# Forgetting attention in a Macaron layer: weight splits moved to the long tiles, a key split in two, and one row of the last stage reordered

## The chip, the cores and the metric

The kernel runs on one core of a Trainium2 chip. The metric is the device time of one execution in microseconds. The program has five engines with a queue of instructions each: PE (TensorE, matmul), DVE (VectorE), ACT (ScalarE), POOL (GpSimd) and SP (SyncE, which here only issues DMAs). Every order below is written out by hand, and the engines meet at semaphores.

## The reference

One layer on 1024 tokens of width 1024, all in float32: a feed-forward block (SwiGLU, inner width 2816), a mixer, a cross attention to 256 memory rows, and a second feed-forward block, each between two RMS norms and with a residual, then a last RMS norm. Half of the mixer is the forgetting attention (8 heads of 64):

```python
def forgetting_attention(q, k, v, log_f):
    qf = (q.astype(F32) * (dh ** -0.5)).transpose(0, 2, 1, 3)
    c = jnp.cumsum(log_f, axis=1).transpose(0, 2, 1)
    for i in range(S // Q_BLOCK):
        s = jnp.einsum('bhqd,bhkd->bhqk', qf[:, :, q0:L], kf[:, :, :L])
        s = s + c[:, :, q0:L, None] - c[:, :, None, :L]
        p = jax.nn.softmax(jnp.where(mask, s, -jnp.inf), axis=-1)
        outs.append(jnp.einsum('bhqk,bhkd->bhqd', p, vf[:, :, :L]))
```

The last block ends with `x = x + 0.5 * rms_norm(y, g_ff2_post)` and `return rms_norm(x, g_final)`.

## The kernel before

Products in float32 are made of three products of rounded parts: a tensor is split into a high part (ACT copies it into the rounded type) and a low part (DVE subtracts the high part from the source). `high_s(n)` (line 952; its copy is line 993) and `low_s(n)` (line 2004; line 2013) do this for the n-th piece of the weights, and `low_s` frees the raw tile that SP then reloads (`load_s`, line 512).

**Attention.** The 8 heads are done in four pairs (`attend_fox(p)`, p = 0 to 3, one function for each engine). A pair has 16 tiles, one for each head of the pair and block of 128 queries, in the order of `FOX_ORDER` (line 36). A tile of block b has (b + 1) x 128 keys, so tiles 0 to 5 are short (128 to 512 keys), 6 to 10 are mixed (640, 384, 768, 512, 896), and 11 to 15 have 640 to 1024. Tile a goes through the engines so: PE makes the scores (lines 1462 to 1465), DVE takes their maximum (line 2058), ACT the exponential with its sum (line 1066), PE transposes the probabilities (line 1476), DVE copies the first four transposed blocks out (line 2072) and ACT the others (line 1073), PE multiplies with the values (line 1487), and DVE scales the result (reciprocal line 2062, product line 2077). In PE's step a stand, in this order, the scores of tile a, the transposes of a - 1, and the values of a - 2; the scores of tile a wait for the exponential of a - 2, because two pairs of PSUM banks are used in turn. In DVE's step a stand the maximum of a, the reciprocal for a - 3, then the copy of a - 1 and the scaling of a - 3.

Into this are woven, for each pair: the second half (keys 512 to 1023) of the pair's keys, whose low parts DVE makes in `keep_q` in step 4 (lines 2029 and 2030, one for each head) and signals on `proj_dve`, for which PE's scores of tile 6 wait (line 1449); the copy of one of these parts, `keep_k1`, in step 7 (line 2037), needed from tile 11 on; and the split of two weight pieces for the next pair, ACT's in steps 4 and 6 and DVE's in steps 6 and 8. PE needs these weights for the projections of the next pair, after its scores of tile 15.

**The last stage.** `ff_2(1)` adds the last products of the second feed-forward block tile by tile (eight tiles of 128 tokens). For tile s of step s, DVE adds the product (`add_y`, line 1934), ACT sums the squares (line 810), POOL makes the root (`root1`, lines 649 and 651), DVE scales by it and adds the old row (`scale_y`, lines 1826 and 1830), ACT sums squares again (line 821), POOL makes the second root (`root2`, lines 656 and 658), and DVE makes the output row (`make_row`, line 1841), which SP sends (line 630). The rows stand in two buffers in turn. `make_row(4, i)` waits for the output of tile i - 2 to have landed (line 1838). DVE's queue in step s is `add_y(s)`, `scale_y(s - 1)`, `make_row(s - 2)`.

Of the kernel before, what the change touches and what calls it, by code (L numbers as in the profile page):

```python
# [7 lines left out]
ALU = mybir.AluOpType  # L8
# [8 lines left out]
NT = T // P  # L17
# [49 lines left out]
S_FV, S_SMALL, S_Q, S_GQ, S_GV, S_GR, S_OUT = 0, 4, 5, 13, 17, 21, 25  # L67
# [41 lines left out]
def build_layer(nc, x, mem, g_ff1_pre, w_ff1_gate, w_ff1_up, w_ff1_down, g_ff1_post,  # L109
# [4 lines left out]
    with ctx:  # L114
# [27 lines left out]
        ps = ctx.enter_context(nc.psum_tensor("ps", [P, 8, HT], F32))  # L142
# [82 lines left out]
        def f32(ap):  # L225
            return ap.bitcast(F32)
# [80 lines left out]
        ka = [at_kb(f"ka{i}", (172, 168)[i], [P, T], F32R) for i in range(2)]  # L307
# [70 lines left out]
        proj_done, proj_dve, proj_act = sem("proj_done"), sem("proj_dve"), sem("proj_act")  # L378
# [417 lines left out]
        def _(act):  # L796
# [248 lines left out]
            def attend_fox(p):  # L1045
                splits = {4: S_Q + 2 + 2 * p, 6: S_Q + 3 + 2 * p}
                for a in range(17):
# [4 lines left out]
                    if a < 16:  # L1052
# [12 lines left out]
                        bank = 2 * (a % 2)  # L1065
# [750 lines left out]
        def _(dve):  # L1816
            ve = nc.vector
# [155 lines left out]
            def ff_2(f):  # L1973
                bd = 1 + 3 * f
# [19 lines left out]
                for s in range(NT + 3):  # L1994
                    if s < NT:
                        add_y(f, NG[f] - 1, s)
                    if 1 <= s <= NT:
                        scale_y(bd, s - 1)
                    if 2 <= s <= NT + 1:
                        make_row(bd, s - 2)  # L2000
                    if f == 0 and s >= 3:
                        low_h(bd, s - 3)
# [12 lines left out]

            def keep_q(n, t, bank):
                dve.wait_ge(proj_done, event(n, t))
# [10 lines left out]
                else:  # L2028
                    ve.tensor_tensor(ka[0][upper, c], ps[lower, bank + t, :], f32(ka[0][lower, c]), ALU.subtract)
                    op = ve.tensor_tensor(ka[1][lower, c], ps[upper, bank + t, :], f32(ka[1][upper, c]), ALU.subtract)  # L2030
                op.then_inc(proj_dve, 1)

# [17 lines left out]
            def attend_fox(p):  # L2050
                splits = {6: S_Q + 2 + 2 * p, 8: S_Q + 3 + 2 * p}
                for a in range(19):
# [7 lines left out]
                    if a >= 3:  # L2060
                        h3, b3 = FOX_ORDER[a - 3]
                        ve.reciprocal(row_inv[:, b3, h3:h3 + 1], row_sum[:, b3, h3:h3 + 1])
                    if a == 4:
                        keep_q(S_Q + 2 * p + 1, 1, 2 if p else 0)
                    if a == 7:
                        keep_k1(p, 1)
# [322 lines left out]
```

## Time and profile before

| | |
|---|---|
| runs | 2337.10, 2337.19, 2345.70 us; median 2337.19 |
| profiled execution | 2339.64 us, of which its span (first to last instruction) 2337.9 us |
| PE busy | 2246.3 us, 96% |
| DVE, ACT, POOL busy | 1117.1 us (48%), 791.0 us (34%), 468.4 us (20%) |
| mean granted clock of PE | 0.979 of 2.4 GHz |
| attention, four pairs | 813.74 to 1074.90 us |
| last stage, tail after the last matmul | 2323.5 to 2337.9 us |

Times in the rows are microseconds from the first instruction of the profiled execution. A row of the timeline gives the start, the duration, engine, line, operation and tiles, and in brackets how long the engine had been idle before it and what ended that. A duration can overlap that of the next row, since the engines are pipelined. A row of a table by stretches gives the stretch, its length, the busy time (and instructions) of PE, of PE's weight loads, of DVE, ACT and POOL, the granted clock of PE (1.00 is 2.4 GHz, 0.50 is 1.2 GHz), the share of the DMA engines and GB/s.

### The profile page before, as it was taken

To read this page: it belongs to the slowest core of one execution; us is meant where nothing else is said; L and a number is where in the kernel's file an instruction comes from. 1 tells how busy PE (TensorE), PEld (TensorE's weight loads), DVE (VectorE), ACT (ScalarE), POOL (GpSimd) and SP (SyncE) were. 2 spreads that over 40 slices of the span, in tenths; PEclk is the share of its full clock that TensorE was granted. 3 is DMA by queue.
4 is the path that set the end of the run, shared out by engine and by line. 5 is a ranking of instruction groups with operands and counts; after the bars stand their busy time and mean duration, and the time that the engine had idled before them with its cause. 6 is when DMAs were issued, how large, how long until landed. Compare 5 with 4: busy or idle time off the path is not lost. (4 is left out here: it accounts for less than half of the span.)

```text
span 2337.9 us, 27140 instructions
## 1 busy us (share of the span) xinstructions
PE 2246.3 (96%) x10640; PEld 1849.0 (79%) x10640; DVE 1117.1 (48%) x1389; ACT 791.0 (34%) x1242; POOL 468.4 (20%) x447
## 2 busy tenths in 40 slices
PE   5999999999999999999999999999699999999997
PEld 4788888888887788888777787778588888888886
DVE  7544444464456354552245543144744444454446
ACT  6433333331124533441222343244533333332113
POOL 2343434300012000000131100001343444410003
PEclk8999999999999996999999999999899999999998
DMA  3222222253333000001131161032122222243323
GB/s 117 91 90 72 90 72 90 73 182 98 117 89 113 19 19 19 20 19 54 55 108 55 58 208 53 16 126 81 45 91 72 90 72 90 79 144 120 117 81 126
DMA packets 105856, 195.01 MB, mean 83 GB/s; under 512 B 8129, under 2 KB 73682, under 8 KB 102914
## 3 DMA queue, kind: packets, MB, share of 16 engines
q1 hardware_dynamic: 105730, 193.27, 25.8%
q8 instruction: 86, 1.41, 0.2%
q14 instruction: 40, 0.33, 0.0%
HBM read 153.34 MB, written 39.91 MB: 83 GB/s over the span
## 5 line engine op out<-in xcount | busy, mean ns | idle before, releaser
L1357 PE MATMUL ps<-xc,wg 128*128 128x512 f32 x1232 | 484.6, 393 | 28.3 <-DVE xc L1892 24.4
L1359 PE MATMUL ps<-xc,wg 128*128 128x512 f32 x1232 | 483.4, 392 | 0.0
L1358 PE MATMUL ps<-xc,wg 128*128 128x512 f32 x1232 | 483.3, 392 | 0.0
L1357 PEld LDWEIGHTS ps<-xc,wg 128*128 128x128 f32 x1232 | 233.9, 190 | 80.4 <-issue 21.9
L1375 PE MATMUL ps<-d_w,d_hid 128*128 128x512 f32 x704 | 274.5, 390 | 2.9 <-DVE d_w L1924 2.8
L1377 PE MATMUL ps<-d_w,d_hid 128*128 128x512 f32 x704 | 273.9, 389 | 0.0
L1376 PE MATMUL ps<-d_w,d_hid 128*128 128x512 f32 x704 | 273.9, 389 | 0.0
L1359 PEld LDWEIGHTS ps<-xc,wg 128*128 128x128 f32 x1232 | 233.5, 189 | 49.1
L1358 PEld LDWEIGHTS ps<-xc,wg 128*128 128x128 f32 x1232 | 233.9, 190 | 48.5
L1898 DVE TENSOR_TENSOR wg<-w_sums,wg 128x1024 fp32r<-128x1024 f32 x88 | 124.1, 1410 | 189.3 <-ACT wg L857 189.3
L1934 DVE TENSOR_TENSOR y<-y,ps 128x1024 f32<-128x1024 f32 x88 | 107.4, 1220 | 215.1 <-PE ps L1377 215.1
L1375 PEld LDWEIGHTS ps<-d_w,d_hid 128*128 128x128 f32 x704 | 132.1, 188 | 31.5 <-DVE d_w L1924 3.7
L863 ACT ACTIVATE fork<-ps 128x512 f32<-128x512 f32 x132 | 78.8, 597 | 228.0 <-PE ps L1359 228.0
L1377 PEld LDWEIGHTS ps<-d_w,d_hid 128*128 128x128 f32 x704 | 132.1, 188 | 27.7
L1376 PEld LDWEIGHTS ps<-d_w,d_hid 128*128 128x128 f32 x704 | 132.2, 188 | 27.0
L1898 DVE TENSOR_TENSOR wg<-w_raw,wg 128x1024 fp32r<-128x1024 f32 x88 | 127.5, 1448 | 49.3 <-ACT wg L857 49.3
L678 POOL TENSOR_TENSOR hid<-hid,up_sum 128x512 f32<-128x512 f32 x66 | 89.2, 1352 | 262.5 <-DVE up_sum L1911 262.5
L1419 PE MATMUL ps<-h_hi,wr 128*128 128x512 f32 x416 | 135.6, 400 | 0.0
L857 ACT ACTIVATE wg<-w_sums 128x1024 fp32r<-128x1024 f32 x88 | 92.9, 1056 | 108.8 <-PE ps L1359 108.1
L649 POOL TENSOR_SCALAR ms<-ss 128x1 f32<-128x1 f32 x32 | 7.4, 232 | 570.6 <-ACT junk L810 570.6
L885 ACT ACTIVATE d_hid<-raw 128x1024 fp32r<-128x1024 f32 x44 | 46.5, 1058 | 210.6 <-PE ps L1377 127.6
L857 ACT ACTIVATE wg<-w_raw 128x1024 fp32r<-128x1024 f32 x88 | 74.2, 844 | 119.9 <-PE ps L1359 119.9
(286 smaller groups left out, 3775.8 us busy)
## 6 DMA issues: line engine op xcount, KB each, us to landing
w_raw<-in_w_ff_gate SPq DMA_DIRECT2D x22, 1024.0 KB, 6.6
w_raw<-in_w_ff_up SPq DMA_DIRECT2D x22, 1024.0 KB, 5.4
hid_dram<-hid SPq DMA_DIRECT2D x22, 1024.0 KB, 4.6
raw<-hid_dram SPq DMA_DIRECT2D x44, 512.0 KB, 3.8
raw<-in_w_ff_down SPq DMA_DIRECT2D x44, 512.0 KB, 3.6
raw<-in_w_mix_in SPq DMA_DIRECT2D x24, 512.0 KB, 3.8
x_row<-x_dram SPq DMA_DIRECT2D x24, 512.0 KB, 4.2
x_dram<-x_ring SPq DMA_DIRECT2D x16, 512.0 KB, 5.0
```

Source lines behind the costliest of these rows:

```text
L678: gp.tensor_tensor(blk, blk, up_sum[:, j, :], ALU.mult).then_inc(hid_done, 1)
L857: sc.activation(group_dst(g, 0), group_src(m, g), ACT.Copy).then_inc(w_hi_done, 1)
L863: sc.activation(fork[:, j, :], ps[:, 3 * (m % 2) + (0, 0, 2)[j], :], ACT.Copy).then_inc(forked, 1)
L1357: mm(acc, hi, x_hi, start=STARTS[q] and k == 0, stop=False, skip_group_check=True)
L1358: mm(acc, hi, x_lo, start=False, stop=False, skip_group_check=True)
L1359: last = mm(acc, lo, x_hi, start=False, stop=k == 3, skip_group_check=True)
L1375: mm(acc, a_hi, b_hi, start=c == 0, stop=False)
L1376: mm(acc, a_hi, b_lo, start=False, stop=False)
L1377: last = mm(acc, a_lo, b_hi, start=False, stop=c == GROUPS[f][gi] - 1)
L1419: last = mm(ps[:, bank, :], w[part // 2][:, i, :], (h_hi, h_lo)[part % 2][:, i, half(t)], start=m == 0, stop=m == 3 * KT - 1, skip_group_c ...
L1898: ve.tensor_tensor(group_dst(g, 1), group_src(m, g), f32(group_dst(g, 0)), ALU.subtract).then_inc(w_lo_done, 1)
L1934: op = ve.tensor_tensor(y[:, i, :], y[:, i, :], two_banks(2 * UNIT_PAIR[u]), ALU.add)
```

## The change

Three edits. In each `attend_fox(p)` the two weight splits move: ACT's from steps 4 and 6 to 9 and 11, DVE's from 6 and 8 to 11 and 13. DVE's two low parts of the late half of the keys, both in step 4 before, stand in steps 4 and 5, with the signal behind the second, and the copy `keep_k1` moves from step 7 to 9. In the last stage (f = 1 only) the row of tile 5 no longer stands behind the scaling of tile 6 but behind that of tile 7, just ahead of the row of tile 6.

```diff
@@ attend_fox, ACT
-                splits = {4: S_Q + 2 + 2 * p, 6: S_Q + 3 + 2 * p}
+                splits = {9: S_Q + 2 + 2 * p, 11: S_Q + 3 + 2 * p}
@@ ff_2, DVE
-                    if 2 <= s <= NT + 1:
+                    if 2 <= s <= NT + 1 and not (f == 1 and s == NT - 1):
+                        if f == 1 and s == NT:
+                            make_row(bd, NT - 3)
                         make_row(bd, s - 2)
@@ keep_q, DVE
-            def keep_q(n, t, bank):
+            def keep_q(n, t, bank, which=(0, 1)):
...
-                    ve.tensor_tensor(ka[0][upper, c], ps[lower, bank + t, :], f32(ka[0][lower, c]), ALU.subtract)
-                    op = ve.tensor_tensor(ka[1][lower, c], ps[upper, bank + t, :], f32(ka[1][upper, c]), ALU.subtract)
-                op.then_inc(proj_dve, 1)
+                    if 0 in which:
+                        ve.tensor_tensor(ka[0][upper, c], ps[lower, bank + t, :], f32(ka[0][lower, c]), ALU.subtract)
+                    if 1 in which:
+                        op = ve.tensor_tensor(ka[1][lower, c], ps[upper, bank + t, :], f32(ka[1][upper, c]), ALU.subtract)
+                if 1 in which:
+                    op.then_inc(proj_dve, 1)
@@ attend_fox, DVE
-                splits = {6: S_Q + 2 + 2 * p, 8: S_Q + 3 + 2 * p}
+                splits = {11: S_Q + 2 + 2 * p, 13: S_Q + 3 + 2 * p}
...
-                    if a == 4:
-                        keep_q(S_Q + 2 * p + 1, 1, 2 if p else 0)
-                    if a == 7:
+                    if a in (4, 5):
+                        keep_q(S_Q + 2 * p + 1, 1, 2 if p else 0, (a - 4,))
+                    if a == 9:
                         keep_k1(p, 1)
```

## Rows read from the trace of the kernel before

**Rows 1.** Busy time by stretch: the second and the third pair of heads, whole.
```profile
875.64:952.10 76.46, 74.94 (x376) 65.16 (x376) 35.28 (x79) 24.67 (x54) 0.00 (x0) 0.75 0.06 15
952.10:1013.55 61.45, 57.76 (x377) 49.83 (x377) 34.80 (x79) 24.57 (x54) 0.00 (x0) 1.00 0.07 19
```

**Rows 2.** Busy time by stretch: low clock in the first and the second pair.
```profile
825.00:831.00 6.00, 5.26 (x23) 4.47 (x23) 5.13 (x12) 1.83 (x5) 0.00 (x0) 0.50 0.31 87
886.00:923.00 37.00, 36.79 (x154) 32.70 (x154) 18.49 (x38) 10.38 (x24) 0.00 (x0) 0.50 0.11 30
```

**Rows 3.** Timeline of PE, third pair, tiles 4 to 8.
```profile
961.66 0.30 PE L1476 MATMUL ps<-ident,probs 128*128 128x128 f32 x1 [1.12 <-DVE probs_t L2072]
...
962.25 0.48 PE L1462 MATMUL ps<-ka,qa 128*128 128x512 f32 x1
...
963.05 0.23 PE L1465 MATMUL ps<-neg_mask,ident_b 128*128 128x128 bf16 x1
...
965.70 0.77 PE L1476 MATMUL ps<-ident,probs 128*128 128x128 f32 x5 [1.53 <-ACT probs L1066]
...
970.54 0.88 PE L1476 MATMUL ps<-ident,probs 128*128 128x128 f32 x6 [0.84 <-ACT probs L1066]
```

**Rows 4.** Timeline of DVE, third pair, steps 4 to 13.
```profile
960.49 0.69 DVE L2030 TENSOR_TENSOR ka<-ps,ka 64x512 fp32r<-64x512 f32 x1
961.22 0.29 DVE L2072 COPY probs_t<-ps 128x128 f32<-128x128 f32 x1
...
962.21 0.27 DVE L2072 COPY probs_t<-ps 128x128 f32<-128x128 f32 x1
...
962.77 1.22 DVE L2013 TENSOR_TENSOR wr<-raw,wr 128x1024 fp32r<-128x1024 f32 x1
963.90 0.82 DVE L2058 TENSOR_REDUCE neg_max<-ps 128x1 f32<-128x640 f32 x1
...
967.38 1.21 DVE L2013 TENSOR_TENSOR wr<-raw,wr 128x1024 fp32r<-128x1024 f32 x1
968.51 0.95 DVE L2058 TENSOR_REDUCE neg_max<-ps 128x1 f32<-128x768 f32 x1
...
975.58 0.82 DVE L2058 TENSOR_REDUCE neg_max<-ps 128x1 f32<-128x640 f32 x1 [0.45 <-PE ps L1465]
...
981.15 0.96 DVE L2058 TENSOR_REDUCE neg_max<-ps 128x1 f32<-128x768 f32 x1 [0.63 <-PE ps L1465]
```

**Rows 5.** Timeline of ACT, third pair, steps 4, 9 and 11.
```profile
959.16 1.05 ACT L993 ACTIVATE wr<-raw 128x1024 fp32r<-128x1024 f32 x1
...
971.00 0.69 ACT L1066 ACTIVATE probs<-ps,neg_max 128x512 f32<-128x512 f32 x1 [0.51 <-DVE neg_max L2058]
...
976.44 0.79 ACT L1066 ACTIVATE probs<-ps,neg_max 128x640 f32<-128x640 f32 x1 [1.21 <-DVE neg_max L2058]
```

**Rows 6.** Timeline of PE, transposes of tile 6, first and second pair.
```profile
826.87 1.33 PE L1476 MATMUL ps<-ident,probs 128*128 128x128 f32 x5 [0.74 <-ACT probs L1066]
...
889.43 1.33 PE L1476 MATMUL ps<-ident,probs 128*128 128x128 f32 x5 [0.21 <-ACT probs L1066]
```

**Rows 7.** Timeline of DVE and POOL, end of the last stage.
```profile
2326.37 1.33 POOL L651 TENSOR_TENSOR rs<-ms,minus_half 128x1 f32<-128x1 f32 x1
2327.22 1.27 DVE L1841 SCALAR_TENSOR_TENSOR h_row<-y,rs,gb 128x1024 f32<-128x1024 f32 x1
...
2328.41 1.27 DVE L1826 SCALAR_TENSOR_TENSOR y<-y,rs,gb 128x1024 f32<-128x1024 f32 x1
...
2331.45 1.28 DVE L1841 SCALAR_TENSOR_TENSOR h_row<-y,rs,gb 128x1024 f32<-128x1024 f32 x1 [0.44 <-POOL rs L658]
...
2332.94 0.55 POOL L658 TENSOR_TENSOR rs<-ms,minus_half 128x1 f32<-128x1 f32 x1
2333.52 1.28 DVE L1841 SCALAR_TENSOR_TENSOR h_row<-y,rs,gb 128x1024 f32<-128x1024 f32 x1 [0.78 <-POOL rs L658]
```

**Rows 8.** Instructions of line 630 (eight output rows): time from issue to landing.
```profile
DMA to landing us min/median/max: 2.6/2.9/2.9
```

## The prediction

> **What bounds the kernel now.** I read the page's busy shares first: PE 96%, everything else at half or less, so only what makes PE wait, or makes it slow, costs time. Then the table by stretches over the four pairs, then the timelines of PE, DVE and ACT in the third pair, and those of the tail behind the last matmul.
>
> In a pair, the short tiles are a chain through the engines and the long ones are PE's. In the third pair PE waits three times: 1.12 us before the transposes of tile 4, for DVE's copy of tile 3; 1.53 us before those of tile 6; 0.84 us before those of tile 8, the last two for ACT's exponential [rows 3]. From tile 8 on PE runs without a gap to the projections. The exponential waits for DVE's maximum, and DVE had a weight split (1.22 and 1.21 us) just ahead of it both times [rows 4]. The fourth pair repeats this.
>
> The second pair shows something bigger: 76.46 us against 61.45 for the third, at a mean clock of 0.75 against 1.00 [rows 1]. PE was granted 1.2 GHz from 886 to 923, while 36.8 of 37 us busy; in the first pair only for some 6 us [rows 2]. The clock fell behind the wait before tile 4 in the first two pairs, and did not behind the same wait in the other two (1.12 us in the third). So the length of that wait does not decide it, and 76.46 - 61.45 = 15.0 us hang on it.
>
> **Part 1: the splits and the keys, third pair.** DVE's steps 4 to 8, worked out anew.
>
> Second key part: before, it ran at 960.49 and the copy of tile 3 at 961.22 [rows 4]. Now the copy takes its place, 0.73 us earlier, at about 960.5. ACT's split (1.05 us at 959.16 [rows 5]) is gone too, so the exponential of tile 4 is no hindrance, and the transposes of tile 4 move from 961.66 to 960.9. But PE's scores of tile 6 wait for the second part, which now stands behind a copy, a scaling, a maximum and a reciprocal: from 961.22 to 962.21, 0.99 us [rows 4]. It starts at 960.49 + 0.99 = 961.5 and ends at 962.2 to 962.3. The scores of tile 6 started at 962.25 [rows 3]. They start at 962.3 now, not earlier: this edit gains nothing by itself. The hole of 1.1 us stays, cut in two, and I price it at 0 (between -0.7, if the chain of tile 5 is what counts, and +0.1).
>
> First split: the scores of tile 6 ended at 963.28 (963.05 + 0.23 [rows 3]) and the maximum began at 963.90, behind the split [rows 4]. Now it begins at 963.4: 0.5 us earlier. Exponential and transposes follow (965.70 becomes 965.2), and so does the copy of tile 6.
>
> Second split: with it gone (and `keep_k1`, 0.4 us), the maximum of tile 8 waits only for its scores. PE makes them behind the transposes of tile 6 (0.77 us) and the values of tile 5, at 966.2 to 967.2. The maximum starts at 967.25 instead of 968.51 [rows 4], its exponential ends at 969.15, and the transposes of tile 8 start at 969.3 instead of 970.54 [rows 3]. From there PE has no gap: the gain is 970.54 - 969.3 = **1.25 us**, and the same in the fourth pair.
>
> First and second pair, at the low clock: PE's waits for the exponential of tile 6 are only 0.74 and 0.21 us [rows 6]. In the second the maximum was not held by the split (its scores ended later), so the gain is 0; in the first 0.5. Sum over four pairs: 1.25 + 1.25 + 0.5 + 0 = **-3.0 us**.
>
> Where the splits go: ACT in step 9 had 0.51 us idle before the exponential (971.00), now more, since the exponential of tile 8 is 1.25 earlier while tile 9's scores come 1.0 earlier; its 1.05 us push that exponential by 0.2, and PE needs it only 0.7 later. In step 11 it had 1.21 idle: covered [rows 5]. DVE had 0.45 and 0.63 us idle before the maxima of steps 11 and 13 [rows 4]; the splits push them by 1.22 - 0.45 = 0.8 and by 0.6. PE takes the transposes of a tile only behind the next tile's scores, which leaves about 0.7 and 0.9 us. So 0 to 0.1 each, and I take 0. If that cover were gone, 4 x (0.8 + 0.6) = +5.6 us. `keep_k1` in step 9 stands before PE needs it in tile 11.
>
> SP: the reloads of the raw tiles wait for DVE's splits, so both come some 11 us later, and the second now stands ahead of the loads of the decay rows for the next pair (they wait for the scores of tiles 12 and 15). Both are needed over 30 us later, in the next pair. Price 0; POOL has nothing in this stretch.
>
> Bounds of part 1: all of PE's waits for exponentials gone, 2 x (1.53 + 0.84) + 0.74 + 0.21 = -5.7; nothing gained and the cover gone, +5.6. I take -3.0, nearest to the rows of tile 8.
>
> **Part 2: the last stage.** The scaling of tile 7 started at 2328.41, behind the row of tile 5 (2327.22); its root was there at 2326.37 + 1.33 = 2327.70 [rows 7]. Scaling and sum took until 2331.45 - 0.44 = 2331.0, so 2.6 us [rows 7]. Now the scaling starts at 2327.75, 0.66 us earlier, and the sum ends at 2330.35. Then the row of tile 5 at 2330.3, the row of tile 6 at 2331.47, which is where it stood before (2331.45). The second root of tile 7 starts at 2331.6, beside the row of tile 6.
>
> POOL's small power took 1.33 us at 2326.37, beside DVE work that reads two tiles, and 0.55 us at 2332.94, with DVE idle [rows 7]. So the root of tile 7 is ready when the row of tile 6 is done, at 2333.5 as before. The 0.66 us are lost here.
>
> And one wait becomes late. The row of tile 7 goes into the buffer of tile 5 and waits for that output to land. Tile 5 is made at 2330.3 to 2331.55 instead of 2327.22, its DMA is issued at 2331.6 and lands 2.6 to 2.9 us later [rows 8], at 2334.2 to 2334.5. The last row started at 2333.52. So it starts 0.7 to 1.0 us later, and its own output, the last thing of the kernel, with it: **+0.9 us** (bounds -0.66, if neither counts, and +1.0).
>
> The Trainium skill, "DMA: Bandwidth & Descriptors", section "Anatomy of one DMA", gives about 2.0 us fixed plus bytes over 436 GB/s for a DMA of another issuing path; for 512 KB that would be an estimate of 3.2 us and would make +1.3 of this part (2331.6 + 3.2 - 2333.52). The trace has 2.6 to 2.9 for just this transfer and is used.
>
> **Sum.** -3.0 + 0.9 = -2.1 us. The profiled execution's own time 2339.64 becomes 2337.5. It stands 2.45 us above the median of the runs, so I take the difference to the median: 2337.19 - 2.1 = **2335.1 us**.
>
> **Rivals.**
> *The clock stays up longer.* If the second pair keeps 2.4 GHz, its 15.0 us go, and it gains 1.25 as the third does: 2335.1 - 16.2 = 2318.9; half of it, 2327. For it: the second hole shrinks from 1.53 to 1.0 us and the third goes. Against: the clock fell right behind the first hole, which stays 1.1 us, and stayed low for 37 us in which PE had hardly a gap.
> *The clock falls in another pair: slower.* Place: the hole before the scores of tile 6 in the third or fourth pair. Price: 15.0 us for a stay as long as the second pair's, and that pair's 1.25: 2351.3; half, 2343. For it: the hole is the same size in all four pairs and only two fell, so the two that did not may now. It decides from about 14 us on, nearly a whole such stay, since 2.1 are gained first.
> *It does not do what it says.* The maxima are held by the scores of tile 6, which do not move, and the pushed maxima of steps 11 and 13 eat the rest: part 1 is 0, and the tail costs 0.9: 2338.1. Against: rows show DVE without idle time ahead of both maxima.
>
> **Chances.** Forecast with the same low clock 0.50; clock better 0.22; clock worse 0.20; no effect in attention 0.08. The runs of the kernel before differ by 8.6 us themselves. About 0.5% (11.7 us) is what a measurement can tell here. Faster than 2325.5 needs most of the first rival: 0.13. Slower than 2348.9 needs a whole further stay: 0.10. The rest, 0.77, is within. The range goes into both clock cases: 2322 to 2349; the forecast's own range is 2331 to 2340.
>
> **What would show it.** In the changed trace: the scores of tile 6 start 10.15 us (962.25 - 952.10) after the pair's first scores at full clock, as before; the transposes of tile 8 start 17.2 us after them, not 18.4; PE has no wait in tiles 11 to 14; a full-clock pair takes 60.2 us; the last row starts with a wait for the output of tile 5, about 0.9 us later than the root allows. Wrong: a wait of PE for an exponential or a copy in tiles 9 to 14, the last row released by POOL, or clock stretches other than 6 and 37 us, which would be the largest term and not one of mine.

## The result and the profile after

The changed kernel takes 2346.43 us (median of 20 runs, 2342.41 to 2356.86), the kernel before beside it 2341.55 us (20 runs, 2332.75 to 2346.91). The ratio is **1.0033, 95% interval 1.0023 to 1.0044**: some 8 us slower, a small loss that is measured, though it is under the 0.5% that the prediction took for what a measurement can tell. 2335.1 us was forecast, a gain of 2.1 us; the measured time lies between 2322 and 2349, but on the other side of the kernel before. The kernel before had 2337.19 us in the three runs that the forecast started from, and has 2341.55 in twenty.

The profiled execution took 2349.82 us, its span 2348.0 us, at a mean granted clock of 0.973 (before: 0.979). All that the prediction worked out of waits came true, and PE still needed longer. The table by stretches, the first three pairs of heads of the changed kernel, and the low clock in its first, third and fourth pair (columns as in [rows 1]):

```profile
813.11:889.22 76.11, 74.30 (x372) 64.48 (x372) 35.05 (x78) 24.79 (x54) 0.00 (x0) 0.75 0.06 15
889.22:949.43 60.21, 57.98 (x377) 49.90 (x377) 34.98 (x79) 24.56 (x54) 0.00 (x0) 1.00 0.07 19
949.43:1014.71 65.28, 63.78 (x377) 55.13 (x377) 35.07 (x79) 24.79 (x54) 0.00 (x0) 0.90 0.07 18
824.00:861.00 37.00, 36.79 (x159) 32.89 (x158) 19.01 (x38) 11.62 (x24) 0.00 (x0) 0.51 0.11 30
959.00:973.00 14.00, 13.19 (x57) 11.46 (x55) 8.20 (x20) 5.33 (x13) 0.00 (x0) 0.52 0.00 1
1028.00:1038.00 10.00, 10.00 (x44) 9.09 (x44) 4.95 (x13) 3.94 (x9) 0.00 (x0) 0.50 0.01 2
```

The second pair answers the third of [rows 1]: at full clock 60.21 us instead of 61.45. But the first pair now takes 76.11 us, and the third lost 5 us as well. The column of the granted clock says why: it is 0.75 and 0.90 in them, and from 824 to 861 PE is busy 36.79 of 37 us at 1.2 GHz. In the kernel before the low clock lay in the first pair (6.8 us) and the second (37.5 us); here it lies in the first (37.5 us), the third (13.7 us) and the fourth (10.2 us).

The changed order inside a full-clock pair, timeline of PE, second pair (first scores at 889.22), against [rows 3]:

```profile
898.07 0.30 PE L1476 MATMUL ps<-ident,probs 128*128 128x128 f32 x1 [0.39 <-DVE probs_t L2077]
...
899.46 0.50 PE L1462 MATMUL ps<-ka,qa 128*128 128x512 f32 x1 [0.61 <-DVE ka L2034]
...
902.35 0.77 PE L1476 MATMUL ps<-ident,probs 128*128 128x128 f32 x5 [0.96 <-ACT probs L1066]
...
906.42 0.87 PE L1476 MATMUL ps<-ident,probs 128*128 128x128 f32 x6
```

The hole of 1.12 us before the transposes of tile 4 is now two, of 0.39 and 0.61 us, with the transposes of tile 4 and the values of tile 3 between them; the hole before tile 6 fell from 1.53 to 0.96 us; the transposes of tile 8, 17.20 us behind the pair's first scores, have no wait left. Behind them there is none to the end of the pair. What PE waited for in tiles 4 and on of all four pairs, from the waits of PE (total us, times, longest), first the changed kernel, then the kernel before:

```profile
PE ps L1462 <- DVE ka L2034: 2.4, 4, 0.6
PE ps L1476 <- ACT probs L1066: 2.3, 4, 1.0
PE ps L1476 <- DVE probs_t L2077: 1.3, 3, 0.5
```

```profile
PE ps L1476 <- ACT probs L1066: 5.7, 6, 1.5
PE ps L1476 <- DVE probs_t L2072: 4.5, 4, 1.1
```

So 6.0 us of waiting instead of 10.2: 4.2 us fewer, in a kernel whose attention took 257.4 us instead of 252.4. (Attention is counted here from the first scores to the end of the last product with the values, in the kernel before 813.74 to 1066.14; the 1074.90 of its table is a later end.)

Where the clock fell in the first pair, timeline of PE and the stretch behind it:

```profile
821.50 0.30 PE L1476 MATMUL ps<-ident,probs 128*128 128x128 f32 x1 [0.38 <-DVE probs_t L2077]
821.88 0.41 PE L1487 MATMUL ps<-v_rows,probs_t 128*128 128x64 f32 x2
822.89 0.80 PE L1462 MATMUL ps<-ka,qa 128*128 128x512 f32 x1 [0.61 <-DVE ka L2034]
```

```profile
823.00:824.00 1.00, 1.00 (x3) 0.81 (x4) 0.44 (x2) 0.00 (x0) 0.00 (x0) 0.50 0.00 0
```

The scores of tile 6 take 0.80 us there instead of 0.50: they are the first matmul at 1.2 GHz, right behind the second piece of the cut hole, and 1.2 GHz lasts until 861. In the third pair the clock falls in the same piece, before the scores of tile 6 at 959.74; in the fourth it falls at 1027.7, in the hole before the transposes of tile 6.

The span is 10.1 us longer. It splits so: attention +5.0; from its end to the last matmul, in code that the change does not touch, +4.9; the tail +0.8; the start -0.6. The two large ones go with the clock, read microsecond by microsecond: in attention PE ran 61.4 us at 1.2 GHz instead of 44.4, and between attention and the last matmul 30.7 us instead of 20.5. What that cost is worked out below, from kernels that keep the clock.

The last rows, timeline of DVE, SP's queue and POOL in the changed kernel, against [rows 7]:

```profile
2339.56 2.48 DVE L1841 SCALAR_TENSOR_TENSOR h_row<-y,rs,gb 128x1024 f32<-128x1024 f32 x2
...
2340.86 4.41 SPq L630 DMA_DIRECT2D out_x<-h_row  x3
...
2342.23 0.55 POOL L658 TENSOR_TENSOR rs<-ms,minus_half 128x1 f32<-128x1 f32 x1
2343.62 1.28 DVE L1841 SCALAR_TENSOR_TENSOR h_row<-y,rs,gb 128x1024 f32<-128x1024 f32 x1 [1.59 <-DMA out_x<-h_row]
```

The root is there at 2342.78, and the last row starts at 2343.62: it waits for the output of tile 5. From the end of the last matmul to the end of the span it is 15.2 us, before 14.4.

### The profile page after: what moved, and what is told of

Read it like the earlier page. It is cut to its first block and busy times, and to the rows that moved or that the text cites. A ratio compares the mean times of both kernels' runs of the same rounds, so it can differ in the third digit from the quotient of the medians.

```text
span 2348.0 us, 27144 instructions
## 1 busy us (share of the span) xinstructions
PE 2258.9 (96%) x10640; PEld 1859.0 (79%) x10640; DVE 1117.1 (48%) x1389; ACT 791.6 (34%) x1242; POOL 475.7 (20%) x447
```

## The experiments

The theory after the comparison: the change gains in every wait what was forecast, and the clock takes it back; the clock falls at the holes of the first tiles. Against it stood that the clock of an execution wanders anyway, that one of the edits costs in another way, and, once the holes were found, that their sizes or their distance from each other decides.

Three tools are used. One edit is made alone or undone. **Fillers** are matmuls that nobody reads, 512 columns wide, put into a hole of PE; they change no result. Here with 2 before the scores of tile 6 (a is 6), 1 before the transposes of tile 4 (a is 5) and 4 before those of tile 6 (a is 7), told below as fillers 1 + 2 + 4, in PE's order:

```diff
+            def filler(n):
+                for _ in range(n):
+                    mm(ps[:, 5, :], qa[0][:, 0:P], ka[0][:, 0:HT], start=True, stop=True, skip_group_check=True)
@@ attend_fox, PE
                 for a in range(18):
+                    if a == 6:
+                        filler(2)
                     if 1 <= a < 16:
                         scores(p, a)
+                    if a in (5, 7):
+                        filler(1 if a == 5 else 4)
                     if 1 <= a <= 16:
                         transpose_probs(p, a - 1)
```

And **padding** is the same matmul, n times, where PE has no hole:

```diff
@@ scores, PE
                 width = (b + 1) * P
+                if a == 15:
+                    for _ in range(7):
+                        mm(ps[:, 2 * (a % 2), :], qa[0][:, 0:P], ka[0][:, 0:HT], start=True, stop=True, skip_group_check=True)
```

All results in one table. The clock is the mean granted clock over the runs of that kernel, beside that of the kernel before on the same chip; the last column is the time at 1.2 GHz inside attention in the profiled execution (changed kernel 61.4, before 44.4).

| kernel | median us | ratio to before, 95% | clock, before's | us at 1.2 GHz |
|---|---|---|---|---|
| tail edit alone | 2339.61 | 1.0008 (0.9990 to 1.0025) | 0.9787, 0.9804 | 58.0 |
| splits alone | 2334.94 | 1.0018 (0.9996 to 1.0040) | 0.9766, 0.9804 | 64.9 |
| keys alone | 2341.99 | 1.0059 (1.0030 to 1.0087) | 0.9736, 0.9804 | 51.2 |
| change, again | 2347.11 | 1.0041 (1.0024 to 1.0058) | 0.9740, 0.9799 | 54.6 |
| change without keys | 2344.48 | 1.0036 (1.0011 to 1.0062) | 0.9753, 0.9799 | 34.1 |
| change without splits | 2342.43 | 1.0050 (1.0017 to 1.0082) | 0.9738, 0.9799 | 105.8 |
| change, fillers 1 + 2 + 4 | 2321.26 | 0.9937 (0.9925 to 0.9949) | 0.9872, 0.9804 | 0 |
| change, fillers 1 + 2 + 0 | 2320.49 | 0.9926 (0.9905 to 0.9946) | 0.9882, 0.9795 | 0 |
| change, fillers 0 + 0 + 4 | 2327.24 | 0.9951 (0.9935 to 0.9968) | 0.9842, 0.9795 | 17.1 |
| change, fillers 1 + 0 + 0 | 2345.45 | 1.0027 (1.0010 to 1.0044) | 0.9773, 0.9793 | 47.8 |
| change, fillers 0 + 2 + 0 | 2325.40 | 0.9945 (0.9923 to 0.9966) | 0.9863, 0.9793 | 0 |
| before, fillers 4 + 0 + 6 | 2327.03 | 0.9960 (0.9944 to 0.9976) | 0.9872, 0.9795 | 0 |
| change without tail edit, fillers 1 + 2 + 0 | 2320.84 | 0.9922 (0.9900 to 0.9944) | 0.9884, 0.9793 | not read |
| splits alone, fillers 4 + 0 + 0 | 2323.03 | 0.9933 (0.9907 to 0.9959) | 0.9870, 0.9793 | 0 |
| change, 7 padding | 2349.71 | 1.0059 (1.0035 to 1.0082) | 0.9750, 0.9795 | 64.9 |
| before, 6 padding | 2355.16 | 1.0069 (1.0045 to 1.0093) | 0.9746, 0.9791 | 68.3 |
| before, 3 padding | 2351.21 | 1.0051 (1.0026 to 1.0076) | 0.9759, 0.9791 | 27.3 |
| change without keys, 6 padding | 2346.40 | 1.0028 (1.0006 to 1.0050) | 0.9782, 0.9791 | 64.9 |

One profiled execution is one draw: "change without keys" shows 34.1 us in its profile and its runs go from 2333.5 to 2355.7 us with clocks of 0.980 to 0.969. So verdicts here rest on the ratios and the mean clocks. A profile tells where the clock fell in that one execution, and no more.

### The three edits, each alone

```diff
@@ tail edit alone: ff_2, DVE
+                    if 2 <= s <= NT + 1 and not (f == 1 and s == NT - 1):
+                        if f == 1 and s == NT:
+                            make_row(bd, NT - 3)
@@ splits alone: attend_fox, ACT and DVE
+                splits = {9: S_Q + 2 + 2 * p, 11: S_Q + 3 + 2 * p}
+                splits = {11: S_Q + 2 + 2 * p, 13: S_Q + 3 + 2 * p}
@@ keys alone: attend_fox, DVE
+                    if a in (4, 5):
+                        keep_q(S_Q + 2 * p + 1, 1, 2 if p else 0, (a - 4,))
+                    if a == 9:
+                        keep_k1(p, 1)
```

> Only the row of tile 5 in the last stage is moved; attention is that of before. The trace after showed a wait of 1.59 us for the output of tile 5 before the last row, and 15.2 us from the last matmul to the end against 14.4. All theories: the same wait of 1.6 us, the tail 0.8 us longer, and the time 0.8 us over before, which the timing can hardly tell from 0. If the slower time of the changed kernel comes from the tail instead of the clock, this one is 5 us or more over before.

> Attention with the weight splits in steps 9 and 11 (ACT) and 11 and 13 (DVE), both key parts still in step 4, keep_k1 in step 7. At full clock a pair should take about 60.2 us against 61.4, PE waiting 1.1 us in one piece before the transposes of tile 4. Theory 1 (the hole before the scores of tile 6 is the same as before, and the clock is lost by how the pairs now follow each other): mean clock falls by about 0.003 and the time is 4 to 8 us over before, as for the whole change. Theory 2 (the clock is lost because the hole was cut in two by the split keys): this one is 2 to 4 us faster than before, its mean clock the same.

> Attention with the two key parts in steps 4 and 5 and keep_k1 in step 9, the weight splits where they were (steps 4 and 6, 6 and 8). A pair at full clock keeps 61.4 us within 0.5. Theory 1 (the pairs' shorter period costs the clock): time and mean clock as before, within 2 us. Theory 2 (the cut hole costs the clock): 5 to 8 us slower, mean clock lower by about 0.003.

The tail edit alone makes no difference that these runs can tell; in its trace the last row waits 1.59 us for the output of tile 5 and the tail takes 15.2 us, as in the changed kernel. Its trace shows one thing more. Its attention is that of the kernel before, and yet PE ran at 1.2 GHz in all four pairs, 58.0 us in all:

```profile
822.00:838.00 16.00, 15.79 (x67) 13.70 (x67) 10.60 (x22) 5.04 (x13) 0.00 (x0) 0.50 0.25 67
890.00:910.00 20.00, 18.84 (x81) 16.75 (x80) 11.80 (x27) 5.79 (x15) 0.00 (x0) 0.50 0.20 53
959.00:964.00 5.00, 4.43 (x19) 3.74 (x18) 4.41 (x11) 1.83 (x5) 0.00 (x0) 0.50 0.40 108
1020.00:1033.00 13.00, 12.79 (x55) 11.21 (x55) 9.57 (x20) 5.08 (x13) 0.00 (x0) 0.50 0.36 83
```

So in which pairs the clock falls, and for how long, is not a property of the order of attention: the profile of the kernel before, with two pairs, is one draw as well.

The splits alone, which should have gained some 3 us, do not (1.0018); their 12 runs stand in two groups, 2332 to 2335 us and 2345 to 2357 us. The keys alone, which cost and gain nothing in the waits, make it 0.6% slower, at the lowest clock of the three. Neither edit of attention is what its waits say.

### Fillers in all holes of the changed kernel

> The changed kernel with extra matmuls of 512 columns in PE's holes, whose results nobody reads: one before the transposes of tile 4, two before the scores of tile 6, four before the transposes of tile 6. At full clock they fit into the holes of 0.4, 0.6 and 0.95 us. If the clock falls because PE does too little around these holes, it stays at 2.4 GHz through all four pairs in nearly all executions: the mean clock rises by 0.01 and the time falls to about 2325, 20 us under the changed kernel. If the clock falls for another reason (the kind of work on the long tiles, or chance), time and clock are as in the changed kernel or some us worse.

The diff is above. 2321.26 us, 1% under the changed kernel (0.9937 against 1.0033), and attention has no microsecond at 1.2 GHz. PE's own work behind the three holes of a pair starts when it did without fillers (second pair: the scores of tile 6 at +10.22 us, in the changed kernel +10.24; the transposes of tile 6 at +13.11 and +13.13); only what PE does in the holes is new. That the clock falls at these holes is shown, and that it is what stood against the change.

### Which hole it is, and the kernel before with fillers

> The changed kernel with fillers in its two first holes only (1 before the transposes of tile 4, 2 before the scores of tile 6); the hole of about 0.96 us before the transposes of tile 6 stays. Theory A (the clock falls behind the first holes): no or little 1.2 GHz in attention, 2321 to 2324 us, ratio to before 0.994. Theory B (the later hole and the short matmuls around it decide): 1.2 GHz for 40 us or more in attention, time as the changed kernel, ratio 1.000 to 1.004. In between, if the holes add up: some 10 to 30 us at 1.2 GHz, ratio about 0.998.

> The changed kernel with fillers only before the transposes of tile 6 (4 of them); the two cut holes of 0.4 and 0.6 us stay. Theory A (the clock falls behind the first holes): as the changed kernel, 40 us or more at 1.2 GHz in attention, ratio 1.000 to 1.004. Theory B (the later hole decides): little or none, ratio 0.994 to 0.995.

> The kernel before, with the same kind of unread 512-column matmuls put into its own holes: 4 before the transposes of tile 4 and 6 before those of tile 6, in each pair (0.21 us each, less than the holes of 1.12 and 1.53 us). What is computed is unchanged. Theory (what PE does in the short tiles decides the clock): no 1.2 GHz inside attention, pairs of about 61.4 us each as the third pair of before; the kernel with the change and fillers had 60.2, and its tail cost 0.8, so this one should take 2321.3 + 4 x 1.25 - 0.8 = 2325 us on the same scale, 0.5% under before. If instead the fillers only worked because the change had already made the holes smaller, the clock still falls here and the time is that of before, 2336, or a little more.

Beside the diff above, first early, then late, then on top of the kernel before:

```diff
-                        filler(1 if a == 5 else 4)
+                        filler(1 if a == 5 else 0)
@@
-                        filler(2)
+                        filler(0)
-                        filler(1 if a == 5 else 4)
+                        filler(0 if a == 5 else 4)
@@
-                        filler(2)
+                        filler(0)
-                        filler(1 if a == 5 else 4)
+                        filler(4 if a == 5 else 6)
```

Three fillers, 0.64 us a pair, do all of it: the hole of 0.96 us before tile 6 stays open and the clock holds. The table by stretches, the second and third pair with the early fillers, then the same pairs of the kernel before with its fillers:

```profile
874.20:934.36 60.16, 58.73 (x379) 50.23 (x380) 34.98 (x79) 24.59 (x54) 0.00 (x0) 1.00 0.07 19
934.36:994.63 60.27, 58.76 (x379) 50.24 (x379) 34.98 (x79) 24.59 (x54) 0.00 (x0) 1.00 0.07 19
```

```profile
875.51:936.96 61.45, 60.15 (x386) 51.41 (x387) 34.81 (x79) 24.60 (x54) 0.00 (x0) 1.00 0.07 19
936.96:998.41 61.45, 60.16 (x386) 51.40 (x386) 34.80 (x79) 24.59 (x54) 0.00 (x0) 1.00 0.07 19
```

With the clock out of the way the change in attention can be read: 61.45 becomes 60.16 and 60.27 (and the first pair 60.99 becomes 59.75), 1.2 to 1.3 us a pair. The whole of attention takes 231.5 us with the change and early fillers and 236.5 us in the kernel before with its fillers, 5.0 us less. Against these two, the low clock had cost 25.9 us in the profile of the changed kernel (257.4) and 15.9 us in that of the kernel before (252.4): 10.0 us more, less the 5.0 gained, are the 5.0 us by which attention got longer there. The ratios of the two filled kernels, 0.9926 and 0.9960, lie 0.34% apart, with intervals of about 0.2% to either side, so they allow the 0.2% of the pairs. So the edits of attention are a gain when the clock is held, and fillers gain 0.4% for the kernel before too. Late fillers alone leave 17.1 us at 1.2 GHz, in short stays of 3.4 to 6.8 us:

```profile
813.05:875.64 62.59, 60.90 (x377) 52.37 (x377) 34.85 (x78) 24.70 (x54) 0.00 (x0) 0.95 0.07 18
875.64:937.20 61.56, 60.30 (x380) 51.87 (x380) 34.98 (x79) 24.70 (x54) 0.00 (x0) 0.97 0.07 18
```

The clock still falls in each of these pairs, but comes back soon. So neither theory as written: with the early holes filled it does not fall, and with the late one filled it falls but stays down for less time.

### Which piece of the cut hole

> The changed kernel with one filler (0.21 us) before the transposes of tile 4, where 0.39 us are idle; the 0.61 us before the scores of tile 6 stay. If the clock falls for the second piece of the cut hole: 1.2 GHz for 30 us or more in attention, ratio 0.999 to 1.004. If for the first: none, 0.993. If for both together: in between.

> The changed kernel with two fillers (0.43 us) before the scores of tile 6, where 0.61 us are idle; the 0.39 us before the transposes of tile 4 stay. If the clock falls for the second piece, which the change newly makes: none or little 1.2 GHz in attention, ratio 0.993 to 0.995. If for the first: 30 us or more, ratio 0.999 to 1.004. If for both together: in between.

Beside the early fillers, the first piece alone, then the second alone:

```diff
-                        filler(2)
+                        filler(0)
@@
-                        filler(1 if a == 5 else 0)
+                        filler(0 if a == 5 else 0)
```

The table by stretches, the first and second pair with the first piece filled, then the same with the second piece filled:

```profile
813.11:888.48 75.37, 73.08 (x374) 63.44 (x374) 34.98 (x78) 24.84 (x54) 0.00 (x0) 0.77 0.06 15
888.48:948.66 60.18, 58.23 (x377) 50.01 (x377) 34.98 (x79) 24.63 (x54) 0.00 (x0) 1.00 0.07 19
```

```profile
817.03:876.74 59.71, 57.57 (x375) 49.39 (x375) 34.76 (x78) 24.62 (x54) 0.00 (x0) 1.00 0.07 19
876.74:936.93 60.19, 58.48 (x378) 50.12 (x378) 34.99 (x79) 24.63 (x54) 0.00 (x0) 1.00 0.07 19
```

With the first piece filled the first pair loses some 15.6 us to the clock, where it lost 16.4 in the changed kernel, and the ratio of 1.0027 can't be told from 1.0033. The clock falls at 825.5 there, 2.6 us behind the unfilled piece, in the hole before the transposes of tile 6. With two fillers, 0.43 us a pair, in the second piece, which the cut of the keys newly makes, no 1.2 GHz is left in attention, and 0.39 us of the first piece and the 0.96 us before tile 6 are still idle.

### Parts of the change with fillers, and a better version

> The changed kernel with fillers in its two first holes (1 and 2, in each pair) but with the last stage as in the kernel before. Theory (the reordered row of the last stage costs about 0.8 us by its wait for an output to land): 0.8 us less than the same kernel with the change's last stage, which had a ratio of 0.9926 and 2320.5 us, so 2319.7 us; the tail from the end of the last matmul to the end of the span 14.4 us instead of 15.2. Rival (the reordering is neutral or gains): 2320.5 us or more, tail 15 us.

> Only the weight splits moved; keys and last stage as in the kernel before; 4 fillers in the one hole before the transposes of tile 4. Theory (splitting the keys' parts gains nothing by itself, and the moved splits give the whole 1.25 us a full-clock pair): no 1.2 GHz in attention, pairs of 60.2 us, 2319.7 us as the kernel with the split keys. Rival (the split keys carry part of the gain): pairs of 60.5 to 60.9 us, 2321 to 2322.5 us. Second rival (a hole in one piece keeps less of the clock than a cut one, even filled): some 1.2 GHz in attention.

The first is the changed kernel with early fillers and this undone; the second has of the change only the two lines of the splits, and fillers 4 + 0 + 0:

```diff
@@ ff_2, DVE
-                    if 2 <= s <= NT + 1 and not (f == 1 and s == NT - 1):
-                        if f == 1 and s == NT:
-                            make_row(bd, NT - 3)
+                    if 2 <= s <= NT + 1:
                         make_row(bd, s - 2)
```

Of the first there is no readable profile, so only its times are used: 2320.84 us, ratio 0.9922, not to be told from the 0.9926 with the tail edit; the 0.8 us that was expected is not shown by them. The tail is read from the second, which has the old order too. Timeline of DVE and POOL:

```profile
2316.07 0.55 POOL L658 TENSOR_TENSOR rs<-ms,minus_half 128x1 f32<-128x1 f32 x1
2316.66 1.28 DVE L1849 SCALAR_TENSOR_TENSOR h_row<-y,rs,gb 128x1024 f32<-128x1024 f32 x1 [0.78 <-POOL rs L658]
```

The last row starts when the root is there, and the tail is 14.5 us (2306.63 to 2321.1); with the tail edit and early fillers the last row waits again, and it is 15.2 us (2304.07 to 2319.3):

```profile
2313.51 0.55 POOL L658 TENSOR_TENSOR rs<-ms,minus_half 128x1 f32<-128x1 f32 x1
2314.91 1.28 DVE L1849 SCALAR_TENSOR_TENSOR h_row<-y,rs,gb 128x1024 f32<-128x1024 f32 x1 [1.60 <-DMA out_x<-h_row]
```

And the splits alone give the whole gain of a pair (its second and third, all at full clock):

```profile
873.76:933.83 60.07, 58.68 (x381) 50.43 (x381) 34.89 (x79) 24.63 (x54) 0.00 (x0) 1.00 0.07 19
933.83:993.93 60.10, 58.73 (x381) 50.42 (x381) 34.88 (x79) 24.62 (x54) 0.00 (x0) 1.00 0.07 19
```

60.07 and 60.10 us are no more than the 60.16 and 60.27 with the cut keys: the cut gains nothing. The best versions (0.9922 to 0.9937) are 0.6 to 0.8% under the kernel before and about 1% under the changed one; among themselves they can't be ranked.

### The same work elsewhere

The diff is the padding shown above.

> Control: the changed kernel with as much unread wide work as the one with fillers (7 matmuls of 512 columns a pair), but among the long tiles, ahead of the scores of tile 15, where PE has no hole. Each costs its 0.21 us, 7 x 4 x 0.21 = 6 us in all. Theory (the holes of the short tiles decide the clock): the low clock stays as in the changed kernel, 50 to 65 us in attention, and the time is the changed kernel's plus 6 us, ratio about 1.006. Rival (any more wide work in a pair keeps the clock up): little 1.2 GHz, 2321 + 6 = 2327 us, ratio 0.996. Second rival (what counts is how the four pairs lie to each other in time, since a pair is as long as in the kernel before again, 61.7 us at full clock): the low clock falls back towards the 44 us of before, ratio 1.002 or less.

Seven of the same matmuls where PE has no hole keep nothing: clock 0.9750, ratio 1.0059, the changed kernel's and the 6 us of their own work. More wide work in a pair is not what holds the clock; its place is. Nor did the clock come back because a pair again lasted as long as in the kernel before.

### One edit undone at a time

```diff
@@ change without keys: attend_fox, DVE
-                    if a in (4, 5):
-                        keep_q(S_Q + 2 * p + 1, 1, 2 if p else 0, (a - 4,))
-                    if a == 9:
+                    if a == 4:
+                        keep_q(S_Q + 2 * p + 1, 1, 2 if p else 0)
+                    if a == 7:
                         keep_k1(p, 1)
@@ change without splits: attend_fox, ACT and DVE
-                splits = {9: S_Q + 2 + 2 * p, 11: S_Q + 3 + 2 * p}
+                splits = {4: S_Q + 2 + 2 * p, 6: S_Q + 3 + 2 * p}
-                splits = {11: S_Q + 2 + 2 * p, 13: S_Q + 3 + 2 * p}
+                splits = {6: S_Q + 2 + 2 * p, 8: S_Q + 3 + 2 * p}
```

> The changed kernel once more, so that the next two are compared with it on one chip. Expected: ratio to before 1.0033 as before (1.002 to 1.005), mean granted clock 0.970 to 0.976 against 0.980 of before.

> The changed kernel with the cut of the keys' low parts undone: both parts in step 4 and the copy in step 7 as in the kernel before; moved splits and last stage stay. Theory (the new second piece of the hole, before the scores of tile 6, is what loses the clock): fewer us at 1.2 GHz than the changed kernel, mean clock over its runs 0.977 or more, ratio 0.999 to 1.001, so 5 to 10 us under the changed kernel. Rival (the moved splits lose the clock, the cut does nothing): as the changed kernel, within 2 us, ratio 1.003.

> The changed kernel with the weight splits back in their old steps; cut of the keys and last stage stay. Theory (the cut loses the clock): ratio 1.006 to 1.008 (the 3 us that the moved splits gain are gone too), mean clock as the changed kernel's or lower. Rival (the moved splits lose it): clock near that of before, 0.979 to 0.981, ratio 1.000 to 1.001.

The change repeats: 1.0041. Then the theory that the cut alone loses the clock falls. Without it the kernel should have come back to 0.999 to 1.001 and 0.977 or more; it has 1.0036 and 0.9753. Without the splits it is 1.0050 at 0.9738. Each edit of attention loses clock by itself, about as much as both, though the moved splits only make holes smaller. How bad it can get, two pairs of the kernel without the splits:

```profile
877.12:953.61 76.49, 75.08 (x377) 65.16 (x377) 35.33 (x79) 24.66 (x54) 0.00 (x0) 0.75 0.06 15
953.61:1028.63 75.02, 72.19 (x377) 62.74 (x377) 35.05 (x79) 24.56 (x54) 0.00 (x0) 0.80 0.06 15
```

### The same holes at another distance

What both edits share is that they move the holes in time. The padding moves them too, and leaves every hole, its size and the work around it as they were.

```diff
@@ scores, PE, in the kernel before (and with 3; and with 6 in the change without keys)
                 width = (b + 1) * P
+                if a == 15:
+                    for _ in range(6):
+                        mm(ps[:, 2 * (a % 2), :], qa[0][:, 0:P], ka[0][:, 0:HT], start=True, stop=True, skip_group_check=True)
```

> The kernel before with 6 unread 512-column matmuls ahead of the scores of tile 15 in each pair, where PE has no hole; nothing else is changed. Holes, their sizes and all work of the short tiles are those of before; only a pair lasts 6 x 0.21 = 1.3 us longer, so the holes of the next pair come later by that. The added work costs 24 x 0.21 = 5.1 us. Theory S (what decides how much clock is lost is also where the holes of the pairs fall in time, so that nearly any shift does as badly as the change): mean granted clock 0.974 to 0.977 instead of 0.980 and 6 to 10 us on top, ratio 1.004 to 1.007. Theory H (the sizes of the holes and what stands between them decide): clock as in before, 0.980, and ratio 1.002.

> The same with 3 matmuls, 0.64 us a pair, 2.6 us in all. Theory S: clock under 0.978, ratio 1.003 or more. Theory H: clock 0.980, ratio 1.001.

> Moved splits and last stage of the change, keys as before, and 6 such matmuls ahead of the scores of tile 15: a full-clock pair lasts 60.1 + 1.3 = 61.4 us as in the kernel before, while the holes keep their new sizes (1.1 and 0.96 us). Without them this kernel had a mean clock of 0.975 and ratio 1.0036. Theory S: the clock comes back to 0.978 to 0.980, ratio 1.002 to 1.003 with the 5.1 us paid. Theory H: the clock stays at 0.975, ratio 1.0058.

The kernel before with 6 padding matmuls a pair: 1.0069 where 1.0022 is their own work. With 3: 1.0051 where 1.0011 is. Their mean clocks are 0.9746 and 0.9759 beside 0.9791, nearly as low as the changed kernel's (0.9740 beside 0.9799). Timeline of PE in the first of them, the hole before the transposes of tile 4 in its second and third pair, and the table by stretches where the clock was low (the second row answers the first hole shown, the third the second):

```profile
888.88 0.30 PE L1479 MATMUL ps<-ident,probs 128*128 128x128 f32 x1 [1.11 <-DVE probs_t L2075]
```

```profile
959.30 0.45 PE L1479 MATMUL ps<-ident,probs 128*128 128x128 f32 x1 [1.11 <-DVE probs_t L2075]
```

```profile
822.00:837.00 15.00, 14.48 (x61) 12.64 (x61) 10.53 (x25) 5.39 (x13) 0.00 (x0) 0.54 0.27 71
890.00:912.00 22.00, 20.73 (x95) 18.57 (x94) 13.05 (x28) 7.23 (x17) 0.00 (x0) 0.53 0.18 48
959.00:973.00 14.00, 13.49 (x57) 11.74 (x57) 10.59 (x25) 5.39 (x13) 0.00 (x0) 0.51 0.28 76
1027.00:1048.00 21.00, 20.02 (x90) 17.89 (x89) 12.80 (x27) 6.78 (x16) 0.00 (x0) 0.51 0.22 51
```

The hole is that of the kernel before, to a hundredth, and what stands around it is the same. The clock falls in all four pairs, and in [rows 2] in two; but that difference shows nothing, since it falls in all four with the tail edit alone too, and the profile with 3 padding has it in two pairs (27.3 us). What counts are the ratios: beyond their own work the paddings cost the kernel before 0.47% and 0.40%, with intervals of 0.24% and 0.25% to either side, though every hole is as it was. So a change that leaves every hole alone can lose clock as the edits did. That it is the distance between the pairs' holes that does it is the reading left, and it is not shown: the padding also moves all that comes later, and where over the runs the clock was lost is not known.

Two other kernels bear on it and do not agree. The change without the keys, whose pair is brought back to about 61.4 us by padding, has a clock of 0.9782 where it had 0.9753 without, and its ratio is 1.0028, though it carries 5.1 us more work than the one with 1.0036; the two intervals overlap, so that is a hint and no more. The changed kernel with 7 padding, whose pair is as long as before again, kept its low clock (0.9750).

## Why the prediction was wrong

**What bounds the kernel, and the three waits of a pair.** Right. PE's wait alone counts, and the weight splits stood ahead of the maxima.

**The keys.** Right as to the waits: the transposes of tile 4 moved forward (8.85 us behind the first scores, before 9.56), the scores of tile 6 did not (10.24, before 10.15; 10.2 forecast), the hole was cut in two. Splits with and without the cut give 60.1 and 60.2 us a pair. What was missed is that an edit worth 0 us in the waits can still cost time: alone it cost 0.6%.

**The splits.** Right: transposes of tile 6 at +13.13 (13.1 forecast), of tile 8 at +17.20 (17.2), no wait of PE behind them, a full-clock pair of 60.21 us (60.2). The cover for the moved splits held. The -1.25 us forecast for the third and fourth pair came in every pair that kept the clock, so with the clock held the splits and keys are worth 5.0 us and not 3.0.

**The last stage.** Right: +0.8 us for the forecast +0.9, the row of tile 7 released by the output of tile 5, POOL's small power 1.54 us beside DVE's work and 0.55 us alone, the 0.66 us lost. As a time of its own it is too small to be measured: 1.0008.

**The step that failed is the clock.** The forecast let the second pair keep its 37 us and the first its 6 us, "the same low clock", with a price of 0 for any move of the holes. That price had no row behind it, and the stays of 6 and 37 us were those of one profiled execution. By the mean clocks of the changed kernel and of the one before on one chip, 0.9740 and 0.9799 of some 2340 us, PE spent about 28 us more at 1.2 GHz: 2 x 2340 x 0.0059. What such a microsecond costs can be read from pairs: 76.11 against 59.75 us for 37.5 us of it, so 0.44 each, and 65.28 against 60.27 for 13.7, so 0.37; behind attention it was 0.48 (4.9 us of span for 10.2 us more of it). That makes, as an estimate, 10 to 13 us of loss, from which the gains in the waits, 5.0 - 0.8 = 4.2 us, are to be taken: 6 to 9 us slower. Measured are 1.0033 and 1.0041, 7.7 and 9.6 us. The sign of the result is that term's.

The rival "the clock falls in another pair" named the mechanism and gave it 0.20. It sized it as a whole further stay or half of one, 2343 to 2351, and 2346 came; in the profiled execution the clock did fall in the third pair at the hole before the scores of tile 6, as it said, and in the fourth too. Its reason stood in the prediction's own text, ahead of the choice: the same hole of 1.1 us had made the clock fall in two pairs and not in the other two, so its length did not decide it. A forecast that moves every hole could not assume that the same ones fall, and the tail edit alone shows that not even an unchanged attention keeps the same ones. The rival "the clock stays up longer" reasoned that smaller holes are kinder, and had 0.22. The experiments speak against it for this kernel: of the edited kernels without fillers, none had a higher mean clock than the one before. The chances also asked only for changes of more than 0.5%, for what "a measurement can tell here"; twenty runs of each kernel told 0.33%, so the sign of a term of a few microseconds was worth a chance of its own.

**What stays open.** That the clock falls at the short tiles' holes is shown, and that its loss outweighs the gain. Why the same hole makes it fall in one pair or one execution and not in another is not known from these runs; nor why the change makes it fall more. Two edits and two paddings of the kernel before all did worse, and one padding of a changed one perhaps better; how far the changed sizes of the holes count beside their changed distance was not separated. And 4.9 of the profiled span's 10.1 us lie behind attention, in unchanged code, with 10.2 us more at 1.2 GHz there; whether that is handed on by the shifted times or chance is open.

## What to carry to other kernels

When the granted clock in a profile falls at short holes of PE in only some of several like stages, a gain in waits of a few microseconds can be smaller than the clock's term, and the clock then gives the sign. Price the clock first, from the stages at either level, and from more than one execution: which stages fall in one profile says little about the next. Here shortening the holes did not keep the clock, and filling them did. Two or three unread wide matmuls in the right holes (0.4 to 0.6 us of PE a pair that was idle anyway) were worth more than all three edits, and only there: the same matmuls elsewhere cost their own time, and in the kernel before 0.4 to 0.5% beyond it.

## What the runs showed of the hardware

- The clock fell behind holes of PE of 0.6 to 1.1 us among short matmuls, and stayed at 1.2 GHz for up to 37.5 us, while PE was 99% busy (36.79 of 37 us).
- A hole of 0.61 us filled for 0.43 us decided it in the changed kernel: 0 instead of 61.4 us at 1.2 GHz in attention, a mean clock over the runs of 0.9863 instead of 0.9740, with 0.39 and 0.96 us of idle time left beside it.
- A microsecond at 1.2 GHz cost 0.37 and 0.44 us in two pairs of the changed kernel, and 0.36 over the attention of the kernel before (15.9 us for 44.4), less than half. Part of PE's waits vanish while it is slow: 0.21 us before the transposes of tile 6 in the third pair, 0.96 in the second at full clock. In the stretch behind attention 10.2 us more of it went with 4.9 us, 0.48 each. The Trainium skill, "TensorE: Matmul & The Clock Gate", section "Terms", puts the penalty at about the throttled time multiplied by the share of the pulses left out, an estimate of 0.50 each at half rate. The traces come near it behind attention, and in attention, with its waits, the measured 0.36 to 0.44 decide.
- With every hole left as it was, 3 or 6 unread matmuls a pair where PE had none cost the kernel before 0.40% and 0.47% beyond their own work, at mean clocks of 0.9759 and 0.9746 beside 0.9791.
- Where the clock falls differs between executions with the same order of attention: 6.8 and 37.5 us in two pairs of the kernel before, and 17.1, 20.5, 6.8 and 13.7 us in the four of the one with the tail edit alone.
- The clock varies between executions of one program: 12 runs of the change without its splits stand in two groups, 2340.2 to 2343.2 us at 0.976 to 0.978, and 2365.3 to 2369.1 us at 0.965 to 0.968.
